# A streaming encoder layer on one core: two banks for projection results, one for turned halves, the first chunk's mask on TensorE, and later places for splits and store waits

## The chip, the cores and the metric

The kernel runs on one core of a Trainium2 chip. A core has a matrix engine (TensorE, PE), a vector engine (DVE), a scalar engine (ACT), a general engine (GpSimd, POOL) and a queue for transfers (SyncE, SP). Results of TensorE land in PSUM, eight banks of 128 partitions x 512 floats. The metric is device time in microseconds, lower is better.

## The reference

One layer for 2048 new frames of a stream and 64 frames of a second, running one, with a cache of 128 past frames. The rows are split into chunks of 512 here, and the whole is:

```python
h = rmsnorm(x, g_mix); proj = h @ w_in            # 1024 -> a, gate, q, k, v (512 each)
u = a * sigmoid(gate)
c = depthwise_conv(u, width 31) + b_dw
c = silu(layernorm(c, g_cn, b_cn)) @ w_pw
q, k = rmsnorm per head (8 heads x 64)
z = q @ k.T / 8;  mask = kpos < qpos              # strictly causal
A = exp(log_sigmoid(z) + sum over later keys of log_sigmoid(-z)),  0 where masked
x = x + concat(c, A @ v) @ w_out
x = x + relu(rmsnorm(x, g_ff) @ w_ff1)^2 @ w_ff2
```
Outputs are y, the new keys and values, and the last 30 inputs of the convolution.

## The kernel before

**Products in parts.** Each operand is split into a high part (a rounded fp32r copy, a cast on ACT) and a low part (the rest, a subtraction on DVE), and each product is three matmuls: high x high, low x high, high x low. In the profile these are L1973 to L1975 (conv and feed-forward projections), L2038 to L2040 (k, v, q) and L2331 to L2333 (output projection).

**Weights.** They come in slabs of 128x1024 through a ring of eight. When a slab is first used it is loaded raw (SP L740), ACT casts it (L1196), DVE subtracts (L1571), and SP stores both parts in w_scratch (L747). Later uses load the parts (L742). A table of ticks sets in which slot each step stands; `split_tick` places ACT's cast, `low_tick` DVE's part. Two slabs hold w_pw.

**Stages.** The projection of chunk 0 runs first. Then comes the front, 92 slots on every engine. On PE, slots 0 to 31 hold the a/gate projection of chunk 1 ("ag" results), and from slot 32 on the twelve results of k, v and q of chunk 1, called events 0 to 11 (k 0 to 3, v 4 to 7, q 8 to 11), four slots and 24 matmuls each. Beside them run the rest of the convolution of chunk 0 ("taps", L1611 on DVE), its layer norm (slots 10 to 21: mean L2128, square csq L1372 on ACT, variance L2135, lnv L1767 on DVE, the first cT_hi L1389 on ACT), the pointwise product with w_pw (slots 22 to 28), and from slot 31 to 57 the attention of chunk 0. Behind the front come out(0), window(0) (feed-forward of chunk 0 beside the attention of chunk 1), and so on.

**Attention.** A piece is 128 queries of a head and up to 512 keys. PE makes the scores z with two matmuls (L2169), DVE takes the minimum of the diagonal block with a table of limits (L1807), ACT makes stay (L1414) and beta (L1415), DVE scans stay (L1819), POOL multiplies (L1142), PE turns beta (L2177), ACT and DVE split it (L1426, L1829), and PE multiplies by v (L2200). Chunk 0 has 32 pieces, all of them with a diagonal block, four a head. q, k and v come from scratch in memory (SP L863, L854).

**k and q of chunk 1.** When an event is through, DVE takes it out of its bank (raw_kq L1668), scales it, ACT and DVE split it into `packed`, PE turns it in two halves of four heads (L2050), ACT copies each half to kqT (L1302), and SP stores it (L837, L839). The turned events are stored in place, so ACT's copy waits for the store of two before. In the front the ag results, the events and the turned halves take banks 0, 1 and 2 in turn, in the order of use; a result waits for the one three before, which is often the event directly before. Events 10 and 11 are turned in out(0) (`OUT_TURN`).

**The wait for stores.** Memory of kqT and of the packed values is used again by the layer norm, so ACT waits for the last stores ahead of csq, step 1 of the norm.

**The opening.** The rows of chunk 0 are scaled on DVE (L1587), turned by PE (L1993) into banks 6 and 7, and split (ACT L1225, DVE L1596); tile i+1 is scaled before the low part of tile i.

## Time and profile before

| | us |
|---|---|
| median of three runs (2829.85 to 2835.32) | 2830.93 |
| the profiled execution | 2836.54 |
| its span in the trace | 2834.8 |
| PE busy | 2706.6 (95%) |
| DVE busy | 1672.9 (59%) |
| ACT busy | 1069.4 (38%) |

The span is the time between the first and the last record of the trace, in one execution; all positions below are in us from its start. Idle time stands in the rows of a timeline in square brackets, with what ended it: `[5.73 <-ACT kqT L1302]` says that the engine did nothing for 5.73 us and that ACT's instruction of line 1302 on kqT let it go. A group says how often an instruction of a line ran, what it took and how long its engine was idle before it. PE's granted clock has two levels, 2.4 GHz (1.00 in the column PEclk) and 1.2 GHz (0.50).

### The profile page before, as it was taken

What the parts mean: (1) busy time and instruction counts of PE and PEld (TensorE: products, weight loads), DVE (VectorE), ACT (ScalarE), POOL (GpSimd) and SP (SyncE); (2) the same over time, 40 slices, a digit from 0 to 9 for tenths busy, and PEclk for the clock granted to TensorE, in tenths of its full rate; (3) what the DMA queues carried; (4) which work ended last, traced back from release to release, by engine and by line L of the source; (5) the groups of instructions that cost most, each with busy time, mean ns of one, the idle gap of its engine ahead of it and who ended that gap; (6) DMA issues with size and microseconds to landing.
All of it is one profiled execution on the core that took longest, in us unless ns stands there. A gap on an engine that the chain in (4) does not pass through costs nothing. (4 is left out here: it accounts for less than half of the span.)

```text
span 2834.8 us, 37422 instructions
## 1 busy us (share of the span) xinstructions
PE 2706.6 (95%) x13872; PEld 2273.7 (80%) x13872; DVE 1672.9 (59%) x2653; ACT 1069.4 (38%) x2144; POOL 453.2 (16%) x460
## 2 busy tenths in 40 slices
PE   7878789999999899999999999999999999999999
PEld 6756677788888788778888797778888887898998
DVE  6986776657773468357775357736888842212222
ACT  4333523456552212345554212244666630221221
POOL 2211210012220011022322002102333310000000
PEclk9999899999999999999999999999999999999999
DMA  9695597777777658465554846854455456353542
GB/s 315 236 342 180 166 357 261 288 254 272 273 264 299 243 197 278 174 246 182 179 185 163 315 166 207 268 208 154 139 189 188 144 178 256 138 204 134 195 162 93
DMA packets 262047, 616.19 MB, mean 217 GB/s; under 512 B 23217, under 2 KB 159409, under 8 KB 213741
## 3 DMA queue, kind: packets, MB, share of 16 engines
q1 hardware_dynamic: 261869, 613.80, 60.8%
q8 instruction: 114, 1.87, 0.3%
q14 instruction: 64, 0.52, 0.1%
HBM read 444.79 MB, written 168.94 MB: 217 GB/s over the span
## 5 line engine op out<-in xcount | busy, mean ns | idle before, releaser
L1973 PE MATMUL ps<-h2T_hi,w_s 128*128 128x512 f32 (+1 forms) x1280 | 465.1, 363 | 7.8 <-DMA w_s<-w_scratch 3.7
L1142 POOL TENSOR_TENSOR beta<-beta,stay 128x512 f32<-128x512 f32 (+3 forms) x328 | 312.9, 954 | 906.6 <-DVE stay L1819 870.6
L1975 PE MATMUL ps<-h2T_hi,w_s 128*128 128x512 f32 (+1 forms) x1280 | 453.8, 355 | 0.0
L1974 PE MATMUL ps<-h2T_lo,w_s 128*128 128x512 f32 (+1 forms) x1280 | 453.7, 354 | 0.0
L1889 DVE TENSOR_TENSOR resid<-ps,resid 128x512 f32<-128x512 f32 x256 | 174.7, 688 | 261.2 <-PE ps L2231 260.6
L1414 ACT ACTIVATE stay<-ps 128x512 f32<-128x512 f32 (+3 forms) x328 | 174.8, 533 | 370.5 <-PE ps L2169 215.2
L2229 PE MATMUL ps<-w_s,hid_hi 128*128 128x512 f32 x768 | 308.5, 402 | 0.0
L2230 PE MATMUL ps<-w_s,hid_lo 128*128 128x512 f32 x768 | 299.9, 390 | 0.0
L2231 PE MATMUL ps<-w_s,hid_hi 128*128 128x512 f32 x768 | 299.8, 390 | 0.0
L1489 ACT ACTIVATE ps<-ps 128x512 f32<-128x512 f32 (+1 forms) x160 | 81.3, 508 | 558.0 <-PE ps L1975 558.0
L1973 PEld LDWEIGHTS ps<-h2T_hi,w_s 128*128 128x128 f32 x1280 | 242.8, 190 | 39.6 <-DMA w_s<-w_scratch 3.8
L1819 DVE TENSOR_TENSOR_SCAN stay<-stay,stay,ones 128x512 f32<-128x512 f32 x192 | 274.5, 1430 | 0.0
L1975 PEld LDWEIGHTS ps<-h2T_hi,w_s 128*128 128x128 f32 x1280 | 242.5, 189 | 32.4
L1974 PEld LDWEIGHTS ps<-h2T_lo,w_s 128*128 128x128 f32 x1280 | 243.1, 190 | 28.0 <-issue 1.0
L1611 DVE SCALAR_TENSOR_TENSOR cacc<-uT,vecs,cacc 128x512 f32<-128x512 f32 (+1 forms) x360 | 260.1, 782 | 1.5
L1899 DVE TENSOR_TENSOR hid_lo<-ps,hid_hi 128x512 fp32r<-128x512 f32 x96 | 66.4, 691 | 272.8 <-ACT hid_hi L1499 272.8
L1829 DVE TENSOR_TENSOR aT_lo<-ps,aT_hi 128x512 fp32r<-128x512 f32 (+3 forms) x328 | 189.9, 579 | 17.2 <-ACT aT_hi L1426 11.7
L2169 PE MATMUL ps<-a_k,a_q 128*128 128x512 f32 (+3 forms) x640 | 183.7, 370 | 10.8 <-DMA a_q<-q_scratch 4.5
L2177 PE MATMUL ps<-ident,beta 128*128 128x128 f32 (+1 forms) x1104 | 176.0, 274 | 15.3 <-DVE aT_lo L1829 14.7
L1426 ACT CAST aT_hi<-ps 128x512 fp32r<-128x512 f32 (+3 forms) x328 | 173.6, 529 | 19.3 <-PE ps L2177 14.7
L2177 PEld LDWEIGHTS ps<-ident,beta 128*128 128x128 f32 (+1 forms) x1104 | 133.9, 141 | 52.6 <-issue 25.3
L1415 ACT ACTIVATE beta<-ps 128x512 f32<-128x512 f32 (+3 forms) x328 | 173.5, 529 | 0.0
(211 smaller groups left out, 5208.6 us busy)
## 6 DMA issues: line engine op xcount, KB each, us to landing
w_s<-w_scratch SPq DMA_DIRECT2D x282, 1024.0 KB, 7.9
w_scratch<-w_s SPq DMA_DIRECT2D x94, 1024.0 KB, 8.9
w_raw<-in_w_ff SPq DMA_DIRECT2D x64, 512.0 KB, 5.5
a_k<-k_scratch SPq DMA_DIRECT2D x80, 256.0 KB, 3.9
a_v<-v_scratch SPq DMA_DIRECT2D x80, 256.0 KB, 4.1
a_q<-q_scratch SPq DMA_DIRECT2D x64, 256.0 KB, 4.6
w_raw<-in_w_in SPq DMA_DIRECT2D x20, 512.0 KB, 7.7
mix_scratch<-ohl SPq DMA_DIRECT2D x66, 128.0 KB, 2.9
```

The lines of the kernel that those rows point to most:

```text
L1142: nc.gpsimd.tensor_tensor(v[0:q.r, 0:n], v[0:q.r, 0:n], stay_of(q.z)[0:q.r, 1:n + 1], ALU.mult).then_inc(s_a, 1)
L1611: nc.vector.scalar_tensor_tensor(out=acc, in0=uT[:, k, tap:tap + wd], scalar=vecs[:, k, tap:tap + 1], in1=acc, op0=ALU.mult, op1=ALU.add). ...
L1819: nc.vector.tensor_tensor_scan(v[0:q.r, 0:q.n][:, ::-1], v[0:q.r, 0:q.n][:, ::-1], ones[0:q.r, 0:1].to_broadcast([q.r, q.n]), init, ALU.mu ...
L1829: ins = nc.vector.tensor_tensor(aT_lo[:, o, 0:full, q.t * P:q.t * P + q.r], bank[:, 0:full * q.r].rearrange("p (a b) -> p a b", a=full), a ...
L1973: nc.tensor.matmul(out, w[0], x[0], start=start, stop=False)
L1974: nc.tensor.matmul(out, w[0], x[1], start=False, stop=False)
L1975: return nc.tensor.matmul(out, w[1], x[0], start=False, stop=stop)
L2169: ins = nc.tensor.matmul(ps[0:q.r, Z_BANK + q.z % 2, 0:q.n], x, a_k[:, k0:k0 + q.n], start=v == 0, stop=v == 1)
L2177: ins = nc.tensor.transpose(ps[0:w, T_BANK + q.z % 2, b * q.r:(b + 1) * q.r], beta[q.z % 4][0:q.r, b * P:b * P + w], ident[0:q.r, 0:q.r])
L2229: nc.tensor.matmul(o, hid_hi[x][:, k, q0:q0 + r], wh[:, c0:c0 + BANK], start=k == 0, stop=False)
L2230: nc.tensor.matmul(o, hid_lo[x][:, k, q0:q0 + r], wh[:, c0:c0 + BANK], start=False, stop=False)
L2231: ins = nc.tensor.matmul(o, hid_hi[x][:, k, q0:q0 + r], wl[:, c0:c0 + BANK], start=False, stop=k == 3)
```

## The change

- **Pointwise slabs split late.** The casts of the two w_pw slabs stand 4.0 ticks ahead of their use on ACT, the subtractions 3.5 ticks ahead on DVE.
- **Banks in the front.** ag results take banks 0 to 2 in turn and wait for the one three before; events take banks 2 and 0 in turn and wait for the event two before; both turned halves of an event take bank 1, the second two slots behind the first, and each waits for the copy of the half before. ACT's copies are split likewise.
- **Events turned in out(0).** Event 9 joins 10 and 11; SP's stores of turned events go out two slots later in the front.
- **Mask of chunk 0.** POOL builds a 128x128 block of 0 and -1e30, ACT casts it and an identity. PE adds their product to the scores' last block, between the two matmuls of a piece. DVE's minimum stays for the later chunks only.
- **Waits for stores.** ACT waits for them at step 7 of the norm, ahead of the first write of cT_hi, for all chunks.
- **Order on SP.** In a slot of the front the weights go behind the stores and the attention's loads.
- **Opening.** The rows of chunk 0 take four pairs of banks (two of them the same), and DVE scales three tiles before the first low part.

```diff
 def split_tick(n):
+    if W[n][:2] == ("pw", 0):
+        return use_of(n)[0] - 4.0
     return max(min(load_tick(n) + SPLIT_LAG, use_of(n)[0] - 2.0), -8.0)
 
 
 def low_tick(n):
+    if W[n][:2] == ("pw", 0):
+        return use_of(n)[0] - 3.5
     return max(min(load_tick(n) + SPLIT_LAG + 1.0, use_of(n)[0] - 1.5), split_tick(n))
...
         def norm_bank(which, c, i, hf):
 
-            return 4 + hf if which else (2 * i + hf) % 3 if c == 1 else 6 + hf
+            return 4 + hf if which else (2 * i + hf) % 3 if c == 1 else (6, 0, 2, 6)[i] + hf if c == 0 else 6 + hf
 
         def norm_back(which, c):
 
-            return 3 if c == 1 and not which else 2
+            return 2 if which or c > 1 else 3 if c else 6
...
-        OUT_TURN, OUT_TURNED = (10, 11), (6, 7)
+        OUT_TURN, OUT_TURNED = (9, 10, 11), (6, 7)
...
-        def front_results():
-            out, evs = [("ag", ev) for ev in range(8)], kvq_events(1)
-            for s in range(len(evs) + 3):
-                if s >= 3 and evs[s - 3][0] != "v" and s - 3 not in OUT_TURN:
-                    out += [("turn", s - 3, q) for q in range(2)]
-                if s < len(evs):
-                    out.append(("event", s))
-            return out
-
-        front_in_order = front_results()
-
-        def front_bank(*what):
-            return front_in_order.index(what) % 3
-
-        def front_free(*what):
-
-            n = front_in_order.index(what) - 3
-            if n < 0:
+        def front_bank(kind, x, q=0):
+            return x % 3 if kind == "ag" else (2, 0)[x % 2] if kind == "event" else 1
+
+        def front_free(kind, x, q=0):
+
+            if kind == "turn":
+                return kqT_ok, 2 * (8 + kvq_events(1)[x][2]) + q
+            if kind == "event":
+                return taken(1, x - 2) if x >= 2 else (ag_u, 8) if x else (ag_sig, 7)
+            if x < 3:
                 return ag_u, 4
-            kind, x = front_in_order[n][:2]
-            if kind == "ag":
-                return (ag_sig if x % 2 else ag_u), 4 + x // 2 + 1
-            if kind == "event":
-                return taken(1, x)
-            return kqT_ok, 2 * (8 + kvq_events(1)[x][2]) + front_in_order[n][2] + 1
+            return (ag_u if x % 2 else ag_sig), 4 + (x - 3) // 2 + 1
 
         def ln_step(c, slot):
 
@@ -955,18 +950,18 @@
 
             def front():
                 for t in range(FRONT):
-                    weights(TICK["win", -1, t])
                     for late in tail_turn(0, t, 2):
                         store_turned(0, late)
                     for s in range(len(kvq_events(1))):
                         if t == event_out(s) + 5:
                             store_kv(1, s)
-                        if t == event_out(s) + 10 and s not in OUT_TURN:
+                        if t == event_out(s) + 12 and s not in OUT_TURN:
...
                     for step in att_steps(0, t):
                         att(0, step)
+                    weights(TICK["win", -1, t])
...
-                    if c == 0 and s in (2, 3):
+                    if c == 0 and 2 <= s < 2 + len(OUT_TURN):
                         store_turned(1, OUT_TURN[s - 2])
...
+            nc.gpsimd.memset(mask_raw[:], 0.0).then_inc(consts, 1)
+            pool.wait_ge(consts, 7)
+            nc.gpsimd.affine_select(out=mask_raw[:], in_=mask_raw[:], compare_op=ALU.is_gt, fill=-1e30, base=0,
+                                    pattern=[[-1, P]], channel_multiplier=1).then_inc(consts, 1)
...
-                        if t == event_out(s) + 9 and sec != "v" and s not in OUT_TURN:
-                            kvq_turned(1, s, [front_bank("turn", s, q) for q in range(2)])
+                        for q in range(2):
+                            if t == event_out(s) + 9 + 2 * q and sec != "v" and s not in OUT_TURN:
+                                kvq_turned(1, s, [front_bank("turn", s)] * 2, (q,))
...
                 if step == 1:
-                    if n == 0:
-                        for m in (2 * nt - 2, 2 * nt - 1):
-                            act.wait_ge(kq_st[m % 2], kq_stores(c, m))
-                        for i in (nt - 2, nt - 1):
-                            act.wait_ge(*value_stored(c, i))
-                        act.wait_ge(vo_out[0], 16 * (2 * c + (nt + 1) // 2))
-                        act.wait_ge(vo_out[1], 16 * (2 * c + 2))
-                    else:
+                    if n:
                         act.wait_ge(yn_ok, CB * lb)
                     for k in range(CB):
                         act.wait_ge(xc_ok, CB * lb + k + 1)
...
+                if step == 7 and n == 0:
+                    for m in (2 * nt - 2, 2 * nt - 1):
+                        act.wait_ge(kq_st[m % 2], kq_stores(c, m))
+                    for i in (nt - 2, nt - 1):
+                        act.wait_ge(*value_stored(c, i))
+                    act.wait_ge(vo_out[0], 16 * (2 * c + (nt + 1) // 2))
+                    act.wait_ge(vo_out[1], 16 * (2 * c + 2))
                 k = step - 7
                 if 0 <= k < CB:
                     act.wait_ge(cm_ok, CB * lb + k + 1)
...
-                if q.diag:
-                    act.wait_ge(z_msk, q.m + 1)
+                if q.diag and q.z >= OPENING:
+                    act.wait_ge(z_msk, q.m + 1 - OPENING)
...
-                if q and q.diag:
+                if q and q.diag and q.z >= OPENING:
...
-            norm_scale(0, 0, 0)
+            for i in range(3):
+                norm_scale(0, 0, i)
             for i in range(4):
-                if i < 3:
-                    norm_scale(0, 0, i + 1)
                 norm_lo(0, 0, i)
+                if i == 0:
+                    norm_scale(0, 0, 3)
+                if i == 1:
+                    splits_until(-2.0)
...
                     if t == att_first(0):
                         pe.wait_ge(pw_lo, CB)
                     for s, (sec, i, m) in enumerate(evs):
-                        if t == KVQ_AT + 4 * (s + 3) and sec != "v" and s not in OUT_TURN:
-                            for q in range(2):
+                        for q in range(2):
+                            if t == event_out(s) + 8 + 2 * q and sec != "v" and s not in OUT_TURN:
                                 pe.wait_ge(*front_free("turn", s, q))
                                 turn_packed(1, s, q, front_bank("turn", s, q))
...
+                if q.z == 0:
+                    pe.wait_ge(consts, 10)
                 if q.z >= 2:
                     pe.wait_ge(s_sg, q.z - 1)
                 for v in range(2):
@@ -2167,6 +2175,8 @@
                     else:
                         x, k0 = a_q[:, q.hp % 3, v, q.t * P:(q.t + 1) * P], q.a0 + kv_place(c, q.head)
                     ins = nc.tensor.matmul(ps[0:q.r, Z_BANK + q.z % 2, 0:q.n], x, a_k[:, k0:k0 + q.n], start=v == 0, stop=v == 1)
+                    if v == 0 and q.z < OPENING:
+                        nc.tensor.matmul(ps[:, Z_BANK + q.z % 2, q.n - P:q.n], ident_r[:], mask_r[:], start=False, stop=False)
                 ins.then_inc(z_ps, 1)
...
-                    pe.wait_ge(kqT_ok, 28)
+                    pe.wait_ge(kqT_ok, 2 * (16 - len(OUT_TURN)))
...
-                        if c == 0 and ev < 2:
+                        if c == 0 and ev < len(OUT_TURN):
                             turn_both(1, OUT_TURN[ev], OUT_TURNED)
```

On ACT and DVE in slots 10 to 13 (kqT: turned events of chunk 0; w_s, w_raw: the w_pw slabs; cacc: the convolution; csq, lnv: the norm). ACT before:

```order
L1302 CAST kqT<-ps 128x512 x2
L1196 CAST w_s<-w_raw 128x1024 x2
L1302 CAST kqT<-ps 128x512 x2
L1239 ACTIVATE sgate_second<-ps 128x512
L1372 ACTIVATE csq<-cacc 128x512 x4
L1375 ACT_TABLE_LOAD
L1375 ACTIVATE lnr<-lnv 128x512
```

and now:

```order
L1301 CAST kqT<-ps 128x512 x2
L1288 CAST packed<-kn 128x8x64
L1301 CAST kqT<-ps 128x512 x4
L1238 ACTIVATE sgate_second<-ps 128x512
L1365 ACTIVATE csq<-cacc 128x512 x4
L1195 CAST w_s<-w_raw 128x1024 x2
L1368 ACT_TABLE_LOAD
L1368 ACTIVATE lnr<-lnv 128x512
```

The two casts of w_raw went from before the last kqT copies to behind the squares. DVE before:

```order
L1682 TENSOR_TENSOR packed<-kn,packed 128x8x64
L1611 SCALAR_TENSOR_TENSOR cacc<-uT,vecs,cacc 128x512 x14
L1571 TENSOR_TENSOR w_s<-w_raw,w_s 128x1024 x2
L1611 SCALAR_TENSOR_TENSOR cacc<-uT,vecs,cacc 128x512 x6
L1617 COPY uT<-uT 128x4x30
L1631 TENSOR_TENSOR uT<-ps,sgate_second 128x512
L1763 SCALAR_TENSOR_TENSOR cacc<-ps,cacc 128x512 x4
L1607 TENSOR_SCALAR cacc_second_67<-uT,vecs 128x512
L1611 SCALAR_TENSOR_TENSOR cacc_second_67<-uT,vecs,cacc_second_67 128x512 x2
L1767 TENSOR_SCALAR lnv<-ps 128x512
L1611 SCALAR_TENSOR_TENSOR cacc_second_67<-uT,vecs,cacc_second_67 128x512 x2
```

and now:

```order
L1685 TENSOR_TENSOR packed<-kn,packed 128x8x64
L1614 SCALAR_TENSOR_TENSOR cacc<-uT,vecs,cacc 128x512 x20
L1620 COPY uT<-uT 128x4x30
L1634 TENSOR_TENSOR uT<-ps,sgate_second 128x512
L1766 SCALAR_TENSOR_TENSOR cacc<-ps,cacc 128x512 x4
L1610 TENSOR_SCALAR cacc_second_69<-uT,vecs 128x512
L1614 SCALAR_TENSOR_TENSOR cacc_second_69<-uT,vecs,cacc_second_69 128x512 x2
L1574 TENSOR_TENSOR w_s<-w_raw,w_s 128x1024 x2
L1770 TENSOR_SCALAR lnv<-ps 128x512
L1614 SCALAR_TENSOR_TENSOR cacc_second_69<-uT,vecs,cacc_second_69 128x512 x2
```

The subtractions went from among the taps of cacc to directly before lnv.

On PE, where the fourth piece of head 0 of chunk 0's attention is scored (a_q, a_k: queries and keys) beside an event. Before:

```order
L2038 MATMUL ps<-w_s,hT_second_hi 128x512
L2039 MATMUL ps<-w_s,hT_second_lo 128x512
L2040 MATMUL ps<-w_s,hT_second_hi 128x512
L2169 MATMUL ps<-a_k,a_q 128x512 x2
L2177 MATMUL ps<-ident,beta_132 128x128
L2038 MATMUL ps<-w_s,hT_second_hi 128x512
L2039 MATMUL ps<-w_s,hT_second_lo 128x512
```

and now:

```order
L2044 MATMUL ps<-w_s,hT_second_hi 128x512
L2045 MATMUL ps<-w_s,hT_second_lo 128x512
L2046 MATMUL ps<-w_s,hT_second_hi 128x512
L2177 MATMUL ps<-a_k,a_q 128x512
L2179 MATMUL ps<-mask_r,ident_r 128x128
L2177 MATMUL ps<-a_k,a_q 128x512
L2187 MATMUL ps<-ident,beta_135 128x128
L2044 MATMUL ps<-w_s,hT_second_hi 128x512
```

The mask's matmul stands between the two of the scores. The scores, turns and projections keep their places. On ACT at the start of out(0) (kqT_late: events of q turned late), before:

```order
L1302 CAST kqT_late_117<-ps 128x512 x2
L1289 CAST packed<-kn 128x8x64 x2
L1196 CAST w_s<-w_raw 128x1024 x4
L1302 CAST kqT_late_116<-ps 128x512 x2
L1302 CAST kqT_late_117<-ps 128x512 x2
L1217 ACTIVATE squares,ssum<-resid 128x1024 x2
```

and now:

```order
L1288 CAST packed<-kn 128x8x64 x2
L1195 CAST w_s<-w_raw 128x1024 x4
L1301 CAST kqT_late_120<-ps 128x512 x2
L1301 CAST kqT_late_119<-ps 128x512 x2
L1301 CAST kqT_late_120<-ps 128x512 x2
L1216 ACTIVATE squares,ssum<-resid 128x1024 x2
```

The copies for event 9 moved from before the last splits to behind them, so three pairs of copies stand ahead of the squares.

## Rows read from the trace of the kernel before

**Rows 1.** page, section 1: engine, busy us (share of the span) x instructions

```profile
PE 2706.6 (95%) x13872; PEld 2273.7 (80%) x13872; DVE 1672.9 (59%) x2653; ACT 1069.4 (38%) x2144; POOL 453.2 (16%) x460
```

**Rows 2.** busy time by stage; columns in the first line

```profile
core 0: us, PE busy (x) PEld busy (x) DVE busy (x) ACT busy (x) POOL busy (x), PEclk, DMA share, GB/s
...
151.00:197.00 46.00, 33.64 (x137) 24.58 (x138) 38.73 (x60) 9.85 (x17) 6.02 (x3) 0.89 0.99 330
...
242.00:297.00 55.00, 41.88 (x209) 33.25 (x208) 38.70 (x77) 24.67 (x69) 16.45 (x20) 0.91 0.54 172
297.00:352.00 55.00, 40.17 (x207) 32.63 (x207) 40.10 (x78) 29.78 (x76) 14.96 (x16) 0.88 0.58 184
352.00:401.00 49.00, 41.26 (x176) 33.32 (x174) 40.12 (x64) 15.57 (x25) 6.87 (x4) 0.90 0.97 325
```

**Rows 3.** PE's waits in 150 to 460 us; total us, times, longest

```profile
engine line waited for: us in total, times, longest us
PE ps L2038 <- DVE raw_kq L1668: 10.5, 3, 4.8
PE ps L2177 <- DVE aT_lo L1829: 9.3, 10, 2.1
...
PE ps L2169 <- DMA a_q<-q_scratch: 4.5, 1, 4.5
```

**Rows 4.** timeline, opening; start, us, engine, line, operation, count, idle before

```profile
12.26 1.29 DVE L1596 TENSOR_TENSOR hT_lo<-ps,hT_hi 128x512 fp32r<-128x512 f32 x2 [1.13 <-ACT hT_hi L1225]
13.47 1.27 DVE L1587 SCALAR_TENSOR_TENSOR xfirst<-xfirst,rstd,g_row 128x1024 f32<-128x1024 f32 x1
...
21.91 1.22 DVE L1571 TENSOR_TENSOR w_s<-w_raw,w_s 128x1024 fp32r<-128x1024 f32 x1
...
12.17 0.55 POOL L1091 TENSOR_TENSOR rstd<-rstd,neghalf 128x1 f32<-128x1 f32 x1
```

**Rows 5.** timeline of PE, first projection and slots 10 to 22

```profile
23.27 0.77 PE L1973 MATMUL ps<-hT_hi,w_s 128*128 128x512 f32 x1 [2.62 <-DVE w_s L1571]
...
186.53 5.85 PE L2128 MATMUL ps<-cacc,ones 128*128 128x512 f32 x8 [5.73 <-ACT kqT L1302]
...
196.88 3.70 PE L2135 MATMUL ps<-csq,ones 128*128 128x512 f32 x8 [1.77 <-ACT csq L1372]
...
216.19 0.50 PE L1973 MATMUL ps<-cT_hi,w_s 128*128 128x512 f32 x1 [1.59 <-DVE cT_lo L1791]
```

**Rows 6.** timeline of ACT, slots 10 to 13

```profile
183.12 1.04 ACT L1196 CAST w_s<-w_raw 128x1024 fp32r<-128x1024 f32 x1 [10.10 <-DMA w_raw<-in_w_pw]
...
185.41 1.07 ACT L1302 CAST kqT<-ps 128x512 fp32r<-128x512 f32 x2
...
196.20 2.19 ACT L1372 ACTIVATE csq<-cacc 128x512 f32<-128x512 f32 x4 [9.22 <-DMA q_scratch<-kqT]
```

**Rows 7.** timeline of DVE, slots 10 to 12

```profile
184.20 2.57 DVE L1571 TENSOR_TENSOR w_s<-w_raw,w_s 128x1024 fp32r<-128x1024 f32 x2 [5.82 <-ACT w_s L1196]
186.68 4.43 DVE L1611 SCALAR_TENSOR_TENSOR cacc<-uT,vecs,cacc 128x512 f32<-128x512 f32 x6
```

**Rows 8.** timeline of SP before the attention

```profile
240.43 4.24 SPq L742 DMA_DIRECT2D w_s<-w_scratch  x4
```

**Rows 9.** timeline of PE in the attention of chunk 0

```profile
263.91 0.22 PE L2200 MATMUL ps<-aT_hi,a_v 128*128 128x128 f32 x1
263.97 0.28 PE L2200 MATMUL ps<-aT_lo,a_v 128*128 128x128 f32 x1
...
275.56 0.28 PE L2200 MATMUL ps<-aT_lo,a_v 128*128 128x128 f32 x1
...
296.07 1.03 PE L2050 MATMUL ps<-ident,packed 128*128 128x128 f32 x8
```

**Rows 10.** DVE's groups in 242 to 352 us, the mask

```profile
L1807 DVE TENSOR_TENSOR ps<-ps,limit 128x128 f32<-128x128 f32 x32 | 9.3, 290 | 11.4 <-PE ps L2169 11.0
```

**Rows 11.** waits of all engines in 0 to 500 us, ACT's largest

```profile
ACT stay L1414 <- DVE ps L1807: 48.9, 28, 5.0
```

**Rows 12.** timeline of PE and ACT in out(0)

```profile
400.69 0.47 PE L2331 MATMUL ps<-w_s,mix_first_hi 128*128 128x512 f32 x1 [1.59 <-DVE raw_kq L1668]
...
430.71 1.06 ACT L1217 ACTIVATE squares<-resid 128x1024 f32<-128x1024 f32 x1 [15.07 <-DVE resid L1921]
```

More of the change, by code:

```diff
@@ L340, in build @@
         limit = place("limit", [P, P])
+        ident_r = place("ident_r", [P, P], F32R)
+        mask_r = place("mask_r", [P, P], F32R)
         neghalf = place("neghalf", [P, 1])
@@ L364, in build @@
         srow = place("srow", [HIST, CC], F32, o_cv + 2 * KIB)
+        mask_raw = place("mask_raw", [P, P], F32, o_cv + 8 * KIB)
         ckT = place("ckT", [P, NH, P], F32R, o_cv + 4 * KIB)
@@ L1297, in kvq_turned @@
                     return
-                if m >= 2:
+                if m >= 2 and 0 in halves_of:
                     act.wait_ge(kq_st[m % 2], kq_stores(c, m - 2))
-                for q in range(2):
+                for q in halves_of:
                     act.wait_ge(kqT_ps, 2 * (8 * c + m) + q + 1)
```

6 lines of the change are left out of this document (4 added, 2 removed).

## The prediction

> **What bounds the kernel now.** I read first how busy each engine is over the whole span [rows 1]: the matrix engine works for 2706.6 of 2834.8 us, so what a change can win is its 128 us of idle time and the time it spends at half clock. Next the table by stages [rows 2], on columns 1, 2, 4 and the clock. In 242 to 352 us, where the attention of chunk 0 runs beside the projection of chunk 1, PE is busy 41.88 + 40.17 = 82.05 of 110 us, at a mean granted clock of 0.91 and 0.88. A stretch at half clock does half of its work, so 0.09 x 55 + 0.12 x 55 = 11.6 us of these 110 are lost to the clock, 28.0 to waiting, and about 72 would do (not all of the half-clock time was busy). In 151 to 197 us PE is busy only 33.64 of 46. Later stages are full, and there the change alters no order but one wait (below). Then I read what PE waited for [rows 3]: in 150 to 460 us, 10.5 us for raw_kq in three waits, 9.3 for aT_lo in ten, 4.5 for a_q in one. The change touches all three kinds. The sum is of gains in three places on one path; since PE leads straight from one to the next, they add.
>
> **Opening.** The normalised rows of chunk 0 get banks (6,7), (0,1), (2,3), (6,7), so TensorE's turns wait no more for hT_lo; on DVE the low parts follow each other, with the fourth scaling (1.27 us) ahead of the second, and the low part of slab 0 goes between. Now the first projection starts at 23.27, held by the low split of w_s that starts at 21.91 behind the last hT_lo [rows 4, 5]. The third scaling, now at 13.47 behind two low parts (1.29), can start when POOL has its rstd, 12.72 [rows 4], and end near 14.1; from there a fourth of 1.27, eight low parts of 0.65 and a split of 1.2 make 7.7, so 21.8, with 0.4 for hand-overs 22.2, 1.0 us earlier. At most the 2.62 that PE waited there can go [rows 5], and at least nothing, since the next slabs wait on DVE's splits and on loads: **1.0 us**, 0 to 2.5. The mask is made once, by POOL and two 128x128 casts on ACT, beside the loads of the first slabs, so it costs nothing; if POOL or ACT were late there, it would be a few tenths.
>
> **Slots 10 to 22.** The mean of the convolution starts at 186.53, after 5.73 us of waiting put down to ACT's kqT copies; those stood behind the splits of the pw slabs on ACT, and the splits behind a load that landed at 183.1 [rows 5, 6]. DVE's last taps stood behind the same splits: it ran out of taps at 178.38, waited 5.82 us, split for 2.57, and did six taps of 0.74 until 191.1 [rows 7]. The mean's last matmul needs the last tap: 192.38. Both splits now come after csq. DVE goes on with the taps at 178.4, ends at 182.5 to 183, and the mean ends near 184.7, 7.7 us earlier. The second half of the gain: csq, its four squares of 0.55 us, started at 196.20, 9.22 us behind a store of kqT that ACT waited for [rows 6]. This wait moves to the first write of cT_hi, so the squares follow the means: they start near 186, and the variance ends near 191 instead of 200.6. Late splits cost there: ACT's two of 1.0 follow csq, ending near 189.4 and 190.4, beside the variance matmuls (3.70 us), and DVE's low parts, 2 x 1.28, end near 191.8 just ahead of lnv, so 0.7 of them stands on the path. The moved wait costs nothing: the first cT_hi comes a whole normalisation behind the squares, after 200, and the stores that csq waited for landed by 196.2 [rows 6]. So the first pw matmul goes from 216.19 to about 207.4 [rows 5]: **8.8 us**, 6 to 10. For the other chunks the same moved wait is worth 0: there csq waits for DVE, and the stores are long done.
>
> **Attention of chunk 0, 242 to 352.** Four things go. (a) a_q: PE waits 4.5 us for a load that SP issued only behind four weight loads, 4.24 us of issuing from 240.43 on; the attention loads now go ahead of the weights of their slot [rows 3, 8]. (b) An event (24 matmuls, six a slot) took its bank in a row of three with turned halves, so it waited for the event directly before; now it has banks 2 and 0 and waits for the one two before. Two of the three waits for raw_kq lie here, 8.7 of the 10.5 us, the longest 4.8, and go [rows 3]; the half clock that follows them is in the 11.6. (c) DVE's 32 minima, 9.3 us, go, with 11.4 us of waiting in front of them, and ACT, which waited 48.9 us in all for them, reads the scores as soon as they stand [rows 10, 11]. (d) In exchange PE gets 32 matmuls 128x128.
> The price of one of these the trace does not show; nearest are the turns, 8 in 1.03 us [rows 9], 0.13 apart. Ends: 0.06, from one 128-wide product of a head to the next (263.91, 263.97), and 0.13, so 1.9 to 4.2 us; I take 3.8, nearer the turns since these are the same shape and change weights each time.
> The Trainium skill ("TensorE: Matmul & The Clock Gate", Back-to-back issue gap) has about 81 ns for a 128-wide matmul with its weight load in a stream; by it an estimate of the masks is 32 x 0.081 = 2.6 us, and the sum would be 1.2 us better. No row here shows it, and the sum goes by the rows.
> How short can the stretch get? PE's floor: 72 + 3.8 = 76. DVE: 78.8 busy now [rows 2], less 9.3, 69.5. The other end: the two heads that ran undisturbed took 11.6 us each (one head's last product starts at 263.97, the next one's at 275.56) [rows 9]; eight of them make 93, with masks on PE 97. Those heads still hold two or three of the ten waits for aT_lo, 0.9 us each [rows 3], which the mask's step (0.29 on DVE and two hand-overs) lengthened. I take the middle of 76 and 97, 87: **23 us**, 12 to 32.
>
> **End of the front, and out(0).** The last event waited for the turn of event 8 and raw_kq; it now takes a free bank, and the turn of event 9 (1.03 us) leaves the front. out(0) starts at 400.69 now [rows 12], after 1.59 for raw_kq; it would be 3.3 us earlier relative to the stretch. Against it: eight transposes more in out(0), 1.04, and on ACT the copy for event 10 waits for the store of event 9, issued on SP within out(0). The squares that stand behind the copies start at 430.71 now, after 15.07 us of waiting for resid [rows 12], and that cover hides the store's wait, or all but 1.5 of it. Net **1.8**, -1 to 4.
> Sum: 1.0 + 8.8 + 23 + 1.8 = 34.6. The profiled run took 2836.54 us with a span of 2834.8; it is 5.6 over the median of the runs, somewhere in the full stages, so I take the sum from the median: 2830.9 - 34.6 = **2796 us**.
>
> **Rivals.** (1) The attention stays tied to the chain ACT, DVE, POOL, PE of a piece: the mask leaves it, but the scan and the hand-overs set the pace, and the heads stay at 11.6. Then the stretch takes 97, the gain there is 13, the sum 24.6: 2806. For it: PE's 9.3 us for aT_lo end that chain; against it: ACT's 48.9 us [rows 3, 11]. (2) The gain is given back in transfers. From 352 to 450 us the DMA engines are full, 0.97 up to 401 [rows 2]; work that comes 33 us earlier meets loads that can't. Then only what PE waits for beyond 450 stays: a net 0 to 10, about 2825. Against it: none of PE's larger waits there is for a transfer [rows 3], and the share before, 0.54 to 0.58, leaves 48 us of free transfer time that earlier issue can use. (3) Slower: all is given back as in (2), and out(0) pays: masks 3.8, turn 1.04, and ACT's copy that waits for event 9's store holds the squares. It decides from where that store lands later than the resid rows are summed, now 30 us into out(0); it is issued behind four resid loads and four w_scratch stores in a full queue, and each us beyond counts. With 2 us of that: 2831 + 6 = 2837. (4) The change does not do what it says in slots 10 to 22: the splits stand before lnv, and DVE's 2.6 us and its wait for ACT's part fall wholly on the path. Gain 5 in place of 8.8, else as forecast: 2800.
> Here a rule speaks against fewer banks. The Trainium skill ("Advanced Engine Details and Errata", Bank Collisions) says that no two engines may use one bank in the same cycle; so with both turned halves in bank 1 the second half may start only when ACT has copied the first. The trace has ACT's copy of a half at 0.54 us [rows 6], and two slots of PE work (12 matmuls 512 wide) lie between the halves, so by the rule nothing is added.
>
> **How the numbers follow.** Forecast (with 4 in it) 0.66, at 2796, own range 2785 to 2803; rival 1 0.20, 2801 to 2812; rival 2 0.08, 2818 to 2831; rival 3 0.03; a better attention than 85 us 0.03. The bounds of the terms, 19 to 48, would reach from 2783 to 2812, and they will not all fall on one side: the range is 2782 to 2812. A measurement of this kernel tells about 0.2% (5.7 us) from no change: faster is below 2825.3. Rival 2 gives half of its chance to faster, 0.04 to same; with 0.01 and 0.03 of rival 3: faster 0.92, same 0.05, slower 0.03.
>
> **What would show it.** Right: the mean's first matmul at 178 to 182 and csq straight behind it; no wait for a_q or raw_kq of over 1 us in the attention; clock at 1.0 through most of it; first projection near 22.2; out(0) starting near 364. Wrong, if the attention lasts over 95 us with waits for aT_lo still 1 to 2 us each (rival 1), if PE waits for w_s or resid by DMA between 370 and 430 (rival 2), if the squares on ACT wait for a q_scratch store (rival 3), or if lnv waits for the splits by over 1.5 us (rival 4).

## The result, and the profile after

| | us |
|---|---|
| before, median of four runs (2829.85 to 2841.6) | 2833.12 |
| changed, median of four runs (2802.34 to 2809.4) | 2807.05 |
| ratio, 95% interval | 0.9904, 0.9881 to 0.9928 |
| changed, profiled execution and its span | 2809.4, 2807.6 |

The kernel is faster by 1.0%: 0.9904 x 2830.93 is 2803.8 on the basis of the forecast, 27 us less in place of the 34.6 forecast. Timed again, beside other runs of before, it took 2807.54 against 2836.37, ratio 0.9896 (0.9882 to 0.9911). Two later executions were slow, one of before beside the median 2836.64 (5424 us) and one with the old round of three banks (6899 us): the medians count them, the ratios do not.

The stages of the changed kernel, in stretches that answer to [rows 2] (columns: us, busy us and instructions of PE, PE's weight loads, DVE, ACT and POOL, then PE's granted clock, share of the DMA engines, GB/s). In 151 to 197 PE works 40.90 us instead of 33.64; in the attention its clock is 0.94 and 0.97 instead of 0.91 and 0.88:

```profile
151.00:197.00 46.00, 40.90 (x178) 30.50 (x177) 43.42 (x68) 17.74 (x27) 6.05 (x4) 1.00 0.99 325
242.00:297.00 55.00, 46.13 (x272) 39.83 (x272) 46.27 (x79) 34.03 (x91) 22.10 (x24) 0.94 0.61 177
297.00:352.00 55.00, 46.51 (x237) 38.77 (x236) 41.35 (x67) 24.94 (x51) 8.62 (x8) 0.97 0.80 269
352.00:401.00 49.00, 42.30 (x184) 34.44 (x183) 35.37 (x54) 10.58 (x16) 6.20 (x3) 0.90 0.99 368
```

Fixed stretches show different work in the two kernels. So I took the start of six pieces of work from the timelines of PE and subtracted; all tables below have these columns. "norm" goes from the first a/gate product of chunk 1 to the first pw product, "attention" from chunk 0's first score to its last product with v, "tail" on to the first product of out(0), "out(0)" on to the first feed-forward product, "rest" to the last instruction's start. "First product" lies within "to chunk 1 (start)", so a sum starts with the latter.

| kernel | first product | to chunk 1 (start) | norm | to attention | attention | tail | out(0) | rest |
|---|---|---|---|---|---|---|---|---|
| before | 23.3 | 158.9 | 57.3 | 26.4 | 109.0 | 49.2 | 57.1 | 2376.9 |
| changed | 20.3 | 157.6 | 47.3 | 26.5 | 93.2 | 45.6 | 59.6 | 2377.7 |
| changed, again | 20.7 | 156.7 | 47.4 | 26.4 | 94.5 | 44.7 | 59.6 | 2376.1 |
| forecast of the difference | -1.1 | -1.0 | -8.8 | 0 | -23 | -3.3 | +1.5 | 0 |
| measured (first profile) | -2.9 | -1.3 | -10.0 | +0.1 | -15.8 | -3.6 | +2.5 | +0.8 |

The spans differ by 27.2 (2834.8 and 2807.6); the stages from "to chunk 1" on add up to that but for rounding. One column is off, the attention. PE's waits from 225 to 375 us (total us, times, longest):

```profile
engine line waited for: us in total, times, longest us
PE ps L2056 <- ACT kqT_second L1301: 9.6, 3, 5.5
PE ps L2177 <- DMA a_k<-k_scratch: 5.9, 1, 5.9
PE ps L2056 <- DVE packed L1685: 4.4, 1, 4.4
PE ps L2341 <- DVE raw_kq L1671: 2.3, 1, 2.3
PE ps L2187 <- DVE aT_lo L1832: 1.7, 3, 0.9
PE ps L2210 <- DVE osb L1851: 0.5, 1, 0.5
```

Against [rows 3] the 9.3 us for aT_lo in ten waits are 1.7 in three, the two waits for raw_kq in the attention are gone, and so is a_q. But two new lines stand on top: 9.6 us for kqT_second, 5.9 for a_k. The first score of the third head waits for keys (start, us, engine, line, operation, tiles, in brackets the idle time before), and what SP issued before them is the same burst of four slab loads as in [rows 8], one slot further:

```profile
234.28 2.24 SPq L737 DMA_DIRECT2D w_s<-w_scratch  x4
236.57 0.44 SPq L849 DMA_DIRECT2D a_k<-k_scratch  x1
```

```profile
250.20 0.45 PE L2177 MATMUL ps<-a_k,a_q 128*128 128x128 f32 x1 [5.92 <-DMA a_k<-k_scratch]
250.45 0.41 PE L2179 MATMUL ps<-mask_r,ident_r 128*128 128x128 f32 x1
```

a_k was issued at 236.57, straight behind four loads of 1 MB, and PE had its first score at 250.20: 13.6 us, where the median of a_k is 3.9 from issue to landing. Meanwhile the DMA engines were full:

```profile
238.00:242.00 4.00, 3.46 (x25) 3.01 (x23) 3.41 (x7) 2.28 (x8) 2.01 (x3) 1.00 1.00 416
242.00:246.00 4.00, 2.29 (x12) 1.64 (x11) 3.02 (x5) 2.97 (x8) 0.99 (x2) 1.00 1.01 429
```

Four slabs of 1 MB at 429 GB/s take 9.8 us (an estimate), and the keys came behind them. The mean share of 0.61 over the long stretch hides this. The second burst of four (SP, 295.35) held a store of the attention's output, which ACT needs landed, and with it the copy of a turned half, for which PE waited 5.53:

```profile
295.35 2.35 SPq L737 DMA_DIRECT2D w_s<-w_scratch  x4
297.75 0.77 SPq L810 DMA_DIRECT2D out<-kn  x1
298.56 0.64 SPq L922 DMA_DIRECT2D mix_scratch<-ohl  x1
```

```profile
311.70 0.40 ACT L1438 CAST ohl<-osb 64x256 fp32r<-64x256 f32 x1 [6.95 <-DMA mix_scratch<-ohl]
312.13 0.49 ACT L1414 ACTIVATE stay<-ps 128x384 f32<-128x384 f32 x1
312.52 0.49 ACT L1415 ACTIVATE beta<-ps 128x384 f32<-128x384 f32 x1
312.89 0.59 ACT L1301 CAST kqT_second<-ps 128x512 fp32r<-128x512 f32 x1
```

```profile
313.53 0.69 PE L2056 MATMUL ps<-ident,packed 128*128 128x128 f32 x2 [5.53 <-ACT kqT_second L1301]
```

The masks stand as said, and can now be priced (start in the first column):

```profile
235.28 0.40 PE L2177 MATMUL ps<-a_k,a_q 128*128 128x512 f32 x1
235.51 0.23 PE L2179 MATMUL ps<-mask_r,ident_r 128*128 128x128 f32 x1
235.57 0.45 PE L2177 MATMUL ps<-a_k,a_q 128*128 128x512 f32 x1
```

From a mask's start to the next matmul's start it is 0.06 here; over all 32 it is 2.46 us, 23 of them at 0.06, eight at 0.11 and one at half clock at 0.21. That is 77 ns each in the mean, though no single one took that.

In slots 10 to 13, against [rows 5 to 7], the mean starts at 177.78 and waits 0.89, for the last tap. The squares, the splits and lnv follow in the order of the change:

```profile
177.78 2.74 PE L2134 MATMUL ps<-cacc,ones 128*128 128x512 f32 x6
181.41 1.13 PE L2134 MATMUL ps<-cacc,ones 128*128 128x512 f32 x2 [0.89 <-DVE cacc L1614]
```

```profile
183.38 2.42 ACT L1365 ACTIVATE csq<-cacc 128x512 f32<-128x512 f32 x4 [7.53 <-DVE cacc L1766]
185.70 1.98 ACT L1195 CAST w_s<-w_raw 128x1024 fp32r<-128x1024 f32 x2
```

```profile
187.08 2.35 DVE L1574 TENSOR_TENSOR w_s<-w_raw,w_s 128x1024 fp32r<-128x1024 f32 x2
189.35 0.68 DVE L1770 TENSOR_SCALAR lnv<-ps 128x512 f32<-128x512 f32 x1
```

```profile
204.90 0.50 PE L1979 MATMUL ps<-cT_hi,w_s 128*128 128x512 f32 x1 [1.59 <-DVE cT_lo L1794]
```

### The profile page after: what moved, and what is told of

It is laid out like the page before. It is cut to its first block and busy times, and to the rows that moved or that the text cites. A ratio compares the mean times of both kernels' runs of the same rounds, so it can differ in the third digit from the quotient of the medians.

```text
span 2807.6 us, 37454 instructions
## 1 busy us (share of the span) xinstructions
PE 2692.8 (96%) x13904; PEld 2267.7 (81%) x13904; DVE 1664.9 (59%) x2621; ACT 1068.9 (38%) x2146; POOL 457.0 (16%) x462
## 5 line engine op out<-in xcount | busy, mean ns | idle before, releaser
L1832 DVE TENSOR_TENSOR aT_lo<-ps,aT_hi 128x512 fp32r<-128x512 f32 (+3 forms) x328 | 189.8, 579 | 14.5 <-ACT aT_hi L1426 8.6
L2241 PEld LDWEIGHTS ps<-w_s,hid_hi 128*128 128x128 f32 x768 | 144.4, 188 | 31.9
```

The source lines that it names most:

```text
L1832: ins = nc.vector.tensor_tensor(aT_lo[:, o, 0:full, q.t * P:q.t * P + q.r], bank[:, 0:full * q.r].rearrange("p (a b) -> p a b", a=full), a ...
L2241: ins = nc.tensor.matmul(o, hid_hi[x][:, k, q0:q0 + r], wl[:, c0:c0 + BANK], start=False, stop=k == 3)
```

## The experiments

The theory, from the trace of the changed kernel: the mask's step on DVE was most of the attention's gain (M); the missing part lies in transfers behind bursts of four slab loads, and the order within a slot can't cure that (D); the banks bring little once the mask is off DVE, because the shared bank makes a wait of its own (also M, with B as the rival). Ratios are against the runs of before on the same chip.

**The mask alone**, in the kernel before:

```diff
+                    if v == 0 and q.z < OPENING:
+                        nc.tensor.matmul(ps[:, Z_BANK + q.z % 2, q.n - P:q.n], ident_r[:], mask_r[:], start=False, stop=False)
...
-                if q and q.diag:
+                if q and q.diag and q.z >= OPENING:
```


> The kernel before with one part of the change: the mask of chunk 0 as 32 matmuls on TensorE instead of 32 minima on DVE. Measured by the attention of chunk 0, from its first score to its last product with v: 109.0 us before, 93.2 changed. Theory M (the mask's step on DVE lengthens the chain of every piece, and that is most of the gain): the waits for aT_lo, 9.3 us before, fall under 3, the event waits for raw_kq stay, the stretch takes 97 to 101, the whole 8 to 12 us less than before. Rival R (the events' waits for their bank hold PE, the chain follows): 105 to 109 and 0 to 4 us less.

Measured: 2824.20 against 2836.37, ratio 0.9953 (0.9935 to 0.9970). The attention took 92.4 us in place of 109.0, a larger gain than theory M had said, and as short as with the whole change. The waits of PE from 240 to 386:

```profile
engine line waited for: us in total, times, longest us
PE ps L2048 <- DVE raw_kq L1678: 8.1, 3, 3.6
...
PE ps L2191 <- DVE aT_lo L1839: 3.4, 5, 1.0
PE ps L2181 <- DMA a_q<-q_scratch: 2.8, 1, 2.8
```

The waits for aT_lo fell from 9.3 to 3.4 (M had said under 3), those for raw_kq from 10.5 only to 8.1. By the medians the whole gained 12 us, by the ratio 13. The four executions lie in two pairs, near 2820 and near 2828; the profiled one is of the lower pair, and its span is 16.3 us shorter (2818.5), although its norm took 60.1 instead of 57.3. What parts the pairs is not shown. The longer norm is probably no effect of the mask, since another kernel without late splits (spread loads in the kernel before, below) took 60.3 too.

**The mask back on DVE**, the rest as changed:

```diff
-                if q and q.diag and q.z >= OPENING:
+                if q and q.diag:
...
-                    if v == 0 and q.z < OPENING:
-                        nc.tensor.matmul(ps[:, Z_BANK + q.z % 2, q.n - P:q.n], ident_r[:], mask_r[:], start=False, stop=False)
```

> The changed kernel with the minima back on DVE and no mask matmuls; banks, places and the rest as changed. Theory M: the attention of chunk 0 grows from 93.2 to 102 to 107 us, waits for aT_lo come back to 6 to 10, the whole is 8 to 13 us slower than the changed kernel. Rival R: 93 to 97 us, 0 to 4 slower.

Measured: 2816.30, ratio 0.9925 (0.9910 to 0.9940), 8.8 us over the changed kernel beside it; the attention took 104.4. So in the attention the mask is worth 16.6 alone and 11.2 with the rest, and the rest (banks, order on SP) 4.6 alone and about nothing behind the mask. For the size theory M holds and the rival is out. One sign of M did not come: the waits for aT_lo were 3.6 us in five, not 6 to 10. PE was busy for 81.5 us of the 104.4 at a mean granted clock of 0.85, changed 75.3 of 93.2 at 0.95. So about 5 of the 11.2 us are idle time of PE and 6 are busy time, at the lower clock.

**Slab loads spread**, the rest as changed:

```diff
 def load_tick(n):
+    if W[n][0] in ("v", "q") and W[n][1] == 1:
+        return TICK["win", -1, (32 if W[n][0] == "v" else 48) + 4 * W[n][2]]
     return use_of(n - RING)[1] if n >= RING else -8.0 + 1.5 * n
```


> The changed kernel, but SP issues the eight slab loads of 1 MB for v and q of chunk 1 one by one, four slots apart (from slots 32 and 48), in place of four in a row at slots 31/32 and 48. Theory D (the missing gain lies in loads and stores of the attention that queue behind four slab loads: PE's wait for a_k of 5.9 at 250.2, ACT's of 6.95 for mix_scratch at 311.7, which holds DVE 5.8 and PE 5.5, and the half clock behind both): both go, the attention takes 79 to 84 instead of 93.2, the whole is 9 to 14 us faster than the changed kernel. Rival C (the shared bank of the turned halves and DVE, busy 0.93 between the stalls, set the pace): the waits turn up elsewhere, 89 to 93 and at most 4 us.

Measured: 2796.47 against 2836.37, ratio 0.9858 (0.9841 to 0.9874), 11.1 us under the changed kernel. The attention took 81.4. PE's waits from 225 to 360:

```profile
engine line waited for: us in total, times, longest us
PE ps L2058 <- DVE packed L1687: 6.9, 1, 6.9
PE ps L2058 <- ACT kqT_second L1303: 4.2, 3, 2.4
PE ps L2189 <- DVE aT_lo L1834: 2.8, 5, 0.9
```

The wait for a_k is gone, kqT_second went from 9.6 to 4.2, and the clock of the attention is 0.98 (0.95 with the bursts):

```profile
227.70:309.00 81.30, 73.66 (x440) 63.13 (x439) 71.45 (x121) 54.00 (x143) 32.60 (x36) 0.98 0.67 208
```

Of the 12 to 13 us that the attention lost, 11.1 stayed; the tail grew by 2 to 3 us, where PE now waits 6.9 in place of 4.4 for DVE's packed. Theory D holds, and rival C (89 to 93) is out. This kernel beats both.

**Slab loads spread in the kernel before:**

> The kernel before with only the slab loads for v and q of chunk 1 issued one by one, four slots apart. Attention of chunk 0: 109.0 us before. Theory D1 (the stalls behind four slab loads were there before the change as well, as the 4.5 us for a_q with its half clock, and can be had without it): 101 to 105 us, the whole 4 to 8 us less than before. Rival D2 (before, the chain through DVE's minima held the attention anyway, so the loads were mostly in time): 106 to 109, at most 3 us less.

Measured: 2830.32 against 2837.33, ratio 0.9975 (0.9961 to 0.9990), 7 us less; the attention took 101.1 instead of 109.0. So D1: the bursts cost 8 us already before the change, and 12 behind it, when less else was in the way.

**The weights first in each slot**, SP's order as before:

```diff
                 for t in range(FRONT):
+                    weights(TICK["win", -1, t])
...
                         att(0, step)
-                    weights(TICK["win", -1, t])
```

> The changed kernel with SP's weights at the front of each slot again. Theory D (the attention's load waits for slab loads issued a slot before, so the order within a slot changes nothing): the wait at the second head stays at 5 to 7 us, the attention within 2 us of 93 to 94.5, the whole within 2. Rival, as the prediction had it: the wait grows by 4.5 or a second one comes, 4 to 8 us slower.

Measured: 2804.96 against 2836.64, ratio 0.9898 (0.9881 to 0.9915), which is the changed kernel's within the measurement. The attention took 93.4. The wait took another shape than the 5 to 7 us that D had said: 2.81 for a_q, and then 8.26 on ACT for the store behind the second burst, behind which PE waited 5.7 for beta:

```profile
240.74 0.69 PE L2177 MATMUL ps<-a_k,a_q 128*128 128x384 f32 x1 [2.81 <-DMA a_q<-q_scratch]
```

```profile
304.99 0.40 ACT L1438 CAST ohl<-osb 64x256 fp32r<-64x256 f32 x1 [8.26 <-DMA mix_scratch<-ohl]
```

The order within a slot is worth nothing that can be measured; four slab loads are in front of what the next slot needs either way.

**The old round of three banks**, the rest as changed:

```diff
-        def front_bank(kind, x, q=0):
-            return x % 3 if kind == "ag" else (2, 0)[x % 2] if kind == "event" else 1
...
+        def front_bank(*what):
+            return front_in_order.index(what) % 3
...
```


> The changed kernel with the old round of three banks for results of the front, both turned halves in one slot again; mask on TensorE, event 9 turned in out(0), SP's order stay. Theory M (with the mask off DVE the banks bring nothing: waits for raw_kq go, waits for kqT_second come, both where DVE is behind): the attention takes 92 to 95 us (93.2 and 94.5 changed), with 5 to 7 us of raw_kq waits in place of 9.6 for kqT_second, the whole within 2 us of the changed kernel. Rival B, as the prediction had it (the two event waits with their half clock are worth 8 us or more by themselves): 99 to 103, 5 to 9 us slower.

Measured: 2812.91 against 2836.64, ratio 0.9927 (0.9907 to 0.9946); the changed kernel has 0.9896 and 0.9904, so 6.5 to 9 us by the ratios, and 3 to 5 by the spans of the profiled runs (2810.9 against 2807.6 and 2805.4). The attention took 96.2 and the tail 47.6, each 2 to 3 us more:

```profile
engine line waited for: us in total, times, longest us
PE ps L2056 <- DVE raw_kq L1683: 8.0, 3, 3.6
PE ps L2189 <- DMA a_k<-k_scratch: 5.6, 1, 5.6
...
PE ps L2199 <- DVE aT_lo L1844: 4.3, 3, 2.9
```

Two of the waits for raw_kq lie in the attention, 3.6 and 2.7 us, in place of 9.6 for kqT_second, as M says; the third, 1.8, is in the tail. For the whole it is what B says, 3 to 9 us, for the attention it is nearer to M. And the attention's part is not shown: with the mask alone, which has the old banks too, the attention took 92.4, less than changed, while kernels whose edits lie elsewhere have 92.4 to 94.5 and once 96.5. The tail's 2 to 3 us stand in both kernels with the mask on TensorE and the old banks, 47.6 here and 47.8 there, against 44.7 to 45.6 changed.

**Event 9 turned in the front**, the rest as changed:

```diff
-        OUT_TURN, OUT_TURNED = (9, 10, 11), (6, 7)
+        OUT_TURN, OUT_TURNED = (10, 11), (6, 7)
```

> The changed kernel with event 9 turned in the front again. Theory E (its turn of 1.04 us only changes its place, and the half clock at the start of out(0) belongs to the wait of 2.3 before it): the last event or out(0) starts 1 to 2.5 us later, out(0) up to the first feed-forward product is 1 to 2.5 us shorter (59.6 changed, 57.1 before), the whole within 2 us. Rival (the late turn made the gain at the end of the front, 3.5 us from the attention's end to out(0)): 3 to 5 us slower.

Measured: 2807.32, ratio 0.9906 (0.9885 to 0.9927), the changed kernel's time within the measurement. The tail is 45.0, so event 9's turn did not make its gain; nor did out(0) start later. But out(0) grew to 61.9 and was not shortened. There the theory is wrong: PE waits 1.70 for a kqT_late copy at 380.69 and 4.38 for the third tile of scaled rows at 420.70, where the changed kernel waits 1.61. Why these waits come is not shown.

**Splits and store wait as before**, the rest as changed, and **the splits alone** (the first of the two hunks):

```diff
 def split_tick(n):
-    if W[n][:2] == ("pw", 0):
-        return use_of(n)[0] - 4.0
...
                 if step == 1:
-                    if n:
+                    if n == 0:
+                        for m in (2 * nt - 2, 2 * nt - 1):
+                            act.wait_ge(kq_st[m % 2], kq_stores(c, m))
```

> The changed kernel with the early splits of w_pw and ACT's wait for stores back at step 1 of the norm. Theory N (the two moves bring what the change gained between the first a/gate product of chunk 1 and the first pw product, 57.3 us before, 47.4 changed): 55 to 58 us there, the whole 7 to 11 us slower than the changed kernel. Rival (the gain comes of DMA transfers that fell otherwise, since the first positions shifted): 47 to 51 and 0 to 4 us.

> The changed kernel with w_pw's splits early again, ACT's wait for stores late. From the first a/gate product of chunk 1 to the first pw product: 47.4 us changed, 55.9 with both moves undone. The prediction's steps: the splits hold the mean by 7.7 and cost 0.7 late, and the store wait would hold the squares by 2 once the mean is earlier. Theory S (both steps needed, the wait is covered when the splits are early): 53 to 55 us, 6 to 8 us slower than the changed kernel. Rival W (the wait for stores is the larger one): 48 to 50 us, 1 to 3 slower.

Measured: 2817.29 (0.9942, 0.9925 to 0.9959) with both undone, norm 55.8; 2814.12 (0.9920, 0.9905 to 0.9934) with early splits and the late store wait, norm 55.2. The wait of the mean came back in both, here with early splits alone:

```profile
183.97 5.76 PE L2130 MATMUL ps<-cacc,ones 128*128 128x512 f32 x8 [5.77 <-ACT kqT L1297]
```

```profile
190.57 0.63 ACT L1361 ACTIVATE csq<-cacc 128x512 f32<-128x512 f32 x1 [6.16 <-DVE cacc L1762]
```

The squares wait for DVE there, no more for a store. So moving the store wait brings only 0.6 of norm as long as the splits are early, and late splits bring 8 when the wait is late. Late splits with the wait early were not run.

For the whole, the splits alone cost 4.5 to 7 us by the ratios, S says 6 to 8. Both undone cost 11 to 13, more than N's 7 to 11 and more than the norm's 8.5: the attention of that kernel took 96.5, with 11.6 us of waits for kqT_second in place of 9.6. The two moves do not touch the attention, and why it was longer is open.

**The old opening**, the rest as changed:

```diff
-            for i in range(3):
-                norm_scale(0, 0, i)
+            norm_scale(0, 0, 0)
             for i in range(4):
+                if i < 3:
+                    norm_scale(0, 0, i + 1)
                 norm_lo(0, 0, i)
...
```

> The changed kernel with the old opening: chunk 0's rows in banks 6 and 7, one scaling ahead. The first product starts at 23.27 before, at 20.3 to 20.7 changed; chunk 1's first a/gate product at 158.9 and 159.6 without it, at 154.3 to 157.6 with it. Theory O (the opening is worth what the start shows, less what half clock and the DVE-bound stretch after it take back): first product at 23.1 to 23.6, the a/gate product of chunk 1 at 158 to 160, the whole 1 to 4 us slower than the changed kernel. Rival (all is taken back): the a/gate product at 155 to 157.5, the whole the same.

Measured: 2808.54, ratio 0.9899 (0.9884 to 0.9914), against 0.9896 with the new one. The first product came at 23.32, chunk 1's first at 159.2, as theory O says; with the new opening ten profiles have 154.3 to 157.6 there. But the attention was done at 325.56 against 324.58 and 324.95: two of the three us were gone by then, and what is left is too small to measure.

Undone one by one, the parts come to 8 to 9 us for the mask, 11 to 13 for splits and store wait, 3 to 9 for the banks and about nothing for SP's order, event 9 and the opening: 22 to 31, beside 27 to 29 for the whole.

**Taps moved out of the attention**, on top of the spread loads:

```diff
-                due = 0 if t < a else 5 * (t - a + 1) // 4 if t < 31 else 25 + (t - 30) // 3 if t < 58 else 34 + 3 * (t - 57) // 2
+                due = 0 if t < a else 5 * (t - a + 1) // 4 if t < 22 else 16 + 2 * (t - 21) if t < 31 else 34 if t < 58 else 34 + 3 * (t - 57) // 2
```


> The changed kernel with spread loads, and with nine to ten taps of chunk 1's convolution (0.74 us each on DVE) moved from slots 31 to 57 to slots 22 to 30. Theory L (with the stalls gone, DVE is the limit of the attention: 81.4 us with spread loads, DVE busy 0.93 of the time between the stalls): the attention takes 74 to 78 us, the taps cost 0 to 3 us in slots 22 to 30, the whole is 2 to 6 us faster than with spread loads alone (2796.5). Rival P (PE with its 71 to 75 us at full clock, or the hand-overs, set it): 79 to 82 and nothing, or slower by the 0 to 3 us.

Measured: 2796.00, ratio 0.9857 (0.9842 to 0.9872), the time of the spread loads alone. The attention took 79.2, which is 2.2 less. The norm took 47.4, 1.4 more, but the other changed kernels with late splits have 45.9 to 47.9:

```profile
230.00:309.20 79.20, 73.32 (x441) 63.02 (x439) 67.77 (x116) 53.93 (x143) 31.91 (x36) 0.98 0.69 213
```

DVE has 3.7 us less to do there and is busy 67.8 of 79.2; PE is busy 73.3. These are five taps and not nine to ten: the attention had only five of chunk 1's taps, and the others that moved came out of the tail. So the test is half as strong as meant. L as stated (74 to 78) falls, and the time is within P's 79 to 82; but DVE gave up 3.7 us and the stretch 2.2, so DVE had a part in it. That PE itself sets the attention now is argued, not shown.

## Why the prediction was right, and where not

The way and the places were right, and the time lies in the stated range. It does not lie in the forecast's own range, 2785 to 2803, and what was mis-sized is the term of the attention. Of the signs that were to show it, the mean's early start and the squares straight behind it came, and the waits for a_q and raw_kq went. The clock did not stay at 1.0 (0.94 and 0.97), and out(0) started at 370.20, not near 364.

**Opening, 1.0 forecast, 1.3 to 2.2 measured at chunk 1.** The way was right, the start was misread: 12.72, at which I let the third scaling begin, is the end of the fourth tile's rstd in [rows 4]. The third scaling, of the third tile, began at 11.88:

```profile
11.88 1.28 DVE L1590 SCALAR_TENSOR_TENSOR xfirst<-xfirst,rstd,g_row 128x1024 f32<-128x1024 f32 x1 [0.72 <-POOL rstd L1086]
13.08 1.28 DVE L1599 TENSOR_TENSOR hT_lo<-ps,hT_hi 128x512 fp32r<-128x512 f32 x2
```

So the first product came at 20.34 and not at 22.2. About 0.9 of these 1.9 us is the misread start; the work behind it took 7.2 us and not 7.7, and the 0.4 for hand-overs did not come. Most of the surplus was given back: the first 13 matmuls went at half pitch (0.43 us from start to start), where before it was the first eight.

**Slots 10 to 22, 8.8 forecast, 10.0 measured.** Step by step: the last tap ended at 181.4 (182.5 to 183 forecast), the squares started at 183.38 (186), the first pw product came at 204.90 (207.4). The low parts ended at 189.4 and lnv began at 189.35, after the variance's 188.7: 0.7 of the path, as forecast. The store wait as "second half of the gain" is only half shown: the run with early splits says that its move is worth 0.6 by itself. That it is worth more behind late splits is argued from csq starting at 183.38, before SP had even issued the last stores (185.93).

**Attention, 23 forecast, 15.8 and 14.5 measured.** This is the term that was mis-sized: 87 us were forecast, 93.2 and 94.5 measured, and with the bursts taken apart 81.4. By its parts:
- (a) failed. "The attention loads now go ahead of the weights of their slot" is true and without effect, as the run with the weights first shows. The loads of the next slot stand behind the burst. I had counted 4.5 us and its half clock as gone; 5.9 us for a_k came instead. I read the wait of [rows 3] as one of SP's issuing (4.24 us), and it is one of the transfers' own 10 us, in which the DMA engines were full.
- (b) half failed. The waits for raw_kq went; I did not ask what waits next. Both halves in one bank make PE wait for ACT's copy, which stands in ACT's order behind the attention, 9.6 us. Of these 5.5 are the wait behind the second burst; with spread loads 4.2 are left. I had dismissed this by counting PE's two slots of work between the halves; ACT was up to 8 us behind: the half turned at 277.08 was copied at 285.03. The Trainium skill ("Advanced Engine Details and Errata", Bank Collisions) says that TensorE, VectorE and ScalarE cannot use one bank in the same partition in the same cycle; no run here let them. The wait would be needed without it: a half is 128x512, a whole bank, so the second half overwrites the first. The banks' net is 3 to 9 us; 2 to 3 in the tail are seen in two kernels, the attention's part is not shown.
- (c) was right: alone the mask took the attention to 92.4, as far as the whole change did. But the way was in part another: the waits for aT_lo hardly differ between mask on DVE and on TensorE with the new banks (3.6 and 1.7), and the clock does (0.85 and 0.95).
- (d) was too dear: 2.46 us for 32, against the 3.8 I took. The Trainium skill's 81 ns for such a matmul in a stream ("TensorE: Matmul & The Clock Gate", Back-to-back issue gap) would have made 2.6, and the measured mean of 77 ns agrees, made of 0.06 and 0.11. The turns at 0.13, which I took as nearest, were misread: the 1.03 us for eight [rows 9] hold the end of the last one. The next instruction started at 296.87, 0.80 behind the first turn, so 0.10 each, and 3.2 for 32.
- The floor of 76 was too high by some us: with spread loads the stretch is 81.4 with PE busy 73.7, masks and some half clock in it. The middle, 87, was too long for the kernel without the bursts and too short for the one with them; that it lies between is luck.

**Tail and out(0), net 1.8 forecast, 1.1 measured.** The tail gave 3.6 (3.3 forecast), out(0) took 2.5 (1.5). The extra turn is 0.8 of it, up to the next instruction's start, and half clock the rest: at the start of out(0) PE has waited 2.31 for raw_kq, and 3.4 us at half clock follow, which cost 1.7.

**The rivals.** Rival 1 named about the right size (stretch 97, sum 24.6) for a wrong reason: the waits for aT_lo that were to stay fell to 1.7 us, and the heads between the bursts took 8.7 and 8.6 us from first score to first score (260.8, 269.5, 278.1), not 11.6. The measured 2803.8 (on the basis of the forecast) and 2807.05 are both in its range of 2801 to 2812. Rival 2 did not come: in 352 to 401 the DMA share rose to 0.99, and the gain stayed, with "rest" at 2377.7 and 2376.1 against 2376.9. But its kind of cause, transfers in a queue, took the missing part in another place, 50 to 100 us earlier, at a mean share of 0.61 and 0.80: a mean over a stretch says nothing of four loads at once. Rival 3 cost nothing, but its sign came. ACT waited for event 9's store, 16.30 us and into the copies in front of the squares:

```profile
401.77 1.07 ACT L1301 CAST kqT_late<-ps 128x512 fp32r<-128x512 f32 x2 [16.30 <-DMA q_scratch<-kqT_late]
402.74 1.07 ACT L1216 ACTIVATE squares<-resid 128x1024 f32<-128x1024 f32 x1
```

DVE had finished the row of resid at 402.70, so the squares stood at most 0.04 us for the copies; the cover that the prediction counted on was used up to the last. Rival 4 did not come. The stated range held because it reached up to rival 1's time. Its own bounds were added wrongly: the low ends 0, 6, 12 and -1 make 17 and not 19, so 2814 and not 2812; and the chances for faster make 0.93, not 0.92.

What stays open: what late splits are worth with an early store wait, how much of the opening's 3 us reaches the end, what the banks are worth in the attention, and how PE, DVE and the hand-overs share in what is left of it with spread loads.

## What to carry to other kernels

When a small load feeds the engine that sets the time, look at what is already in the transfer queue at its issue, not at the order of issue within a step: here eight loads of 1 MB, spread over the slots that had time for them, gave 11 us. When a wait is taken away by giving results other banks, write down for each bank who empties it and where that stands in that engine's order; the next wait is there. And a mask on TensorE beside products that it must make anyway cost 2.5 us, and freed 9 us of DVE and two hand-overs of each piece.

## What the runs showed of the hardware

A 128x128 matmul of 128 columns between two matmuls of the same accumulation takes 0.06 us of PE's stream at full clock in 23 of 32 places, and 0.11 in eight. Turns of 128 columns, eight in a row, took 0.10 each by the same measure (from start to start), nearer than the 0.13 of the prediction. And four slab loads of 1 MB issued within 2.2 us of one another fill the DMA engines (1.00 and 1.01 of them in 238 to 246 us, at 416 and 429 GB/s), so PE had a load of 256 KB issued behind them only after 13.6 us, though the mean share of the long stretch around it is 0.61.
